# FFN2 and FFN3 as seven half-block products a unit, with weight sums on GpSimd

## What is computed

```python
# FFN2: D_FF = 2816 (22 tiles of 128)
x = _residual(x, _swiglu(_modnorm(x, g[4], m[6], m[7]), ffn2_w1, ffn2_w3, ffn2_w2), g[5], m[8], 0.5)
def _swiglu(h, w1, w3, w2):
    return (jax.nn.silu(h @ w1) * (h @ w3)) @ w2
...
# FFN3: D_FF_2 = 4096 (32 tiles)
u = rmsnorm(x, norm_mlp_g) @ w_up
x = x + jnp.square(jax.nn.relu(u)) @ w_down
```

## Time and profile before

| | |
|---|---|
| runs | 3321.23, 3317.41, 3318.78 us (median 3318.78) |
| span of the profiled execution | 3320.6 us |
| PE busy | 3122.6 us, 94%, 9082 matmuls |
| PE weight load busy | 1592.1 us, 48% |
| DVE, ACT, POOL busy | 766.2, 433.0, 56.2 us |
| PE L281 `normed` x ring | 4208 matmuls, 1648.2 us |
| PE L281 `big` x ring | 2368 matmuls, 950.3 us |
| HBM | 68 GB/s over the span |

### The profile page before, as it was taken

One profiled execution on the slowest core, in us unless ns is written; L12 is line 12 of the kernel. 1 busy time (PEld: TensorE's weight loads), 2 busy tenths in 40 slices (PEclk: granted clock), 3 DMA queues, 4 the chain that ended last, 5 costly groups with the idle time before them and its releaser, 6 DMA issues.

```text
span 3320.6 us, 22877 instructions
## 1 busy us (share of the span) xinstructions
PE 3122.6 (94%) x9082; PEld 1592.1 (48%) x9082; DVE 766.2 (23%) x1393; ACT 433.0 (13%) x908; POOL 56.2 (2%) x98
## 2 busy tenths in 40 slices
PE   3999999997999999998999998997889999999998
PEld 1555555553557366443444443753434444444443
DVE  6222225004016443002000004108540001110012
ACT  2000000002014243002000001004330001000001
POOL 0000000000002000000000000000000000000000
PEclk8999999998999999998999999998899999999999
DMA  5222223111110100221221121110012121222211
GB/s 244 89 102 103 103 95 144 44 60 38 51 39 1 39 10 29 76 83 51 76 76 72 64 80 63 64 65 13 26 45 76 76 76 64 76 76 76 75 45 57
DMA packets 38460, 227.69 MB, mean 69 GB/s; under 512 B 4208, under 2 KB 4464, under 8 KB 20848
## 3 DMA queue, kind: packets, MB, share of 16 engines
q1 hardware_dynamic: 28736, 181.17, 14.7%
q0 software_dynamic: 8928, 39.85, 3.2%
q10 hardware_dynamic: 720, 5.61, 0.4%
HBM read 224.51 MB, written 2.10 MB: 68 GB/s over the span
## 4 chain that ended last, share of the span: by engine, by line
PE 90%; DVE 6%; ACT 1%; DMA 1%; issue 1%; ACTq 0%; DVEq 0%
PE banks L281 80%; PE banks L386 1%; PE banks L541 1%; PE banks L461 1%; PE banks L534 1%; DMA consts_sb<-consts 1%; PE banks L333 1%; PE banks L290 1%; PE banks L679 1%; DVE rstd L1065 1%; DVE scratch_b L1082 1%; PE banks L451 1%; DVE p_embed L1115 1%; DVE stat L1370 0%; DVE residual L1088 0%
## 5 line engine op out<-in xcount | busy, mean ns | idle before, releaser
L281 PE MATMUL banks<-normed,weight_ring 128*128 128x512 f32 (+3 forms) x4208 | 1648.2, 553 | 53.4 <-ACT normed L769 34.0
L281 PEld LDWEIGHTS banks<-normed,weight_ring 128*128 128x128 f32 (+2 forms) x4208 | 802.4, 191 | 887.9 <-issue 841.0
L281 PE MATMUL banks<-big,weight_ring 128*128 128x512 f32 (+3 forms) x2368 | 950.3, 559 | 11.7 <-DVE big L1168 5.6
L281 PEld LDWEIGHTS banks<-big,weight_ring 128*128 128x128 f32 (+2 forms) x2368 | 444.5, 188 | 506.7 <-issue 480.5
L1115 DVE CUSTOM_DVE_ANT_0 p_embed<-big,rpb_rows 128x1024 f32<-128x1024 f32 x116 | 141.9, 1223 | 22.9 <-DMA big<-w_ada 15.5
L290 PE MATMUL banks<-scratch_a,consts_sb 128*128 128x512 f32 (+1 forms) x124 | 60.1, 621 | 65.5 <-ACT scratch_a L753 64.6
L782 ACT ACTIVATE scratch_b<-banks 128x512 f32<-128x512 f32 x44 | 26.3, 597 | 712.9 <-PE banks L281 712.9
L1075 DVE RECIPROCAL rstd<-rstd 128x512 f32<-128x512 f32 (+1 forms) x3 | 11.7, 3886 | 422.4 <-ACT rstd L757 422.4
L1165 DVE TENSOR_TENSOR scratch_a<-scratch_a,banks 128x512 f32<-128x512 f32 x16 | 11.0, 687 | 356.9 <-ACT scratch_a L815 356.9
L1143 DVE TENSOR_TENSOR big<-scratch_b,banks 128x512 f32 x22 | 15.1, 688 | 314.7 <-ACT scratch_b L782 314.7
L1148 DVE TENSOR_TENSOR big<-scratch_b,banks 128x512 f32 x22 | 15.1, 687 | 288.0 <-ACT scratch_b L782 288.0
(11 more groups left out here) (203 smaller groups left out, 1554.2 us busy)
## 6 DMA issues: line engine op xcount, KB each, us to landing
weight_ring<-weights SPq DMA_DIRECT2D x128, 1024.0 KB, 4.8
weight_ring<-weights SPq DMA_DIRECT2D x32, 704.0 KB, 3.9
big<-w_ada POOLq DMA_DIRECT2D x42, 512.0 KB, 3.9
weight_ring<-weights SPq DMA_DIRECT2D x16, 768.0 KB, 4.1
big<-w_ada POOLq DMA_DIRECT2D x4, 2048.0 KB, 25.1
rpb_rows<-w_ada POOLq DMA_DIRECT2D x14, 512.0 KB, 4.4
weight_ring<-weights SPq DMA_DIRECT2D x8, 640.0 KB, 3.9
residual<-xT ACTq DMA_DIRECT2D x2, 1536.0 KB, 19.7
```

The source lines that it names most:

```text
L281: ins = nc.tensor.matmul(o, w, r, start=start, stop=stop)
```

## The change

Each pair of output tiles of FFN2's and FFN3's products is made by Strassen's scheme in Winograd's form. The weights of a unit are four blocks (two output tiles by two halves of the inner channels, `kp` = 4 tiles each, or 3 in the last four units of FFN2's down product), the rows four blocks (two halves of the channels by two halves of 256 tokens). Seven products of `kp` matmuls of 256 columns stand where eight stood. There are 66 such units: 22 + 12 in FFN2 and 16 + 16 in FFN3.

- GpSimd makes the four sums of weight blocks of each unit (`weight_sums`, 128 x 512 elements each) into two sets of buffers.
- DVE makes the four sums of row blocks once for eight row tiles (`row_sums`, 4 x 256 elements a partition each), nine times in all.
- PE (`fast`) accumulates the seven products in three half banks a unit, with two sets in turn. ACT copies the first product (`fast_snap`), DVE adds the copy to what the second and the fourth left, and PE's products 4, 6 and 7 wait for these adds.
- The inner channels are cut into phases of eight hidden tiles (six at FFN2's end): up for a phase, then down for it, the partial results summed in SBUF (`Y1`, `Y2`, or straight into `X`).
- The last down units' results are squared in pairs of tiles, and PE sums them by four matmuls.
- SP's list (`STREAM`) gives the units in the new order, and a down unit gathers its blocks from two or four of the stored ones; the stored weights are the same.

```diff
+            def fast(v, rows, t, rows_sem=None, rows_at=0, t_at=None):
+
+                n, kp = unit_of(v)
+                za, zb, zc = zones(v)
+                a = [slot(n, i * kp * P, kp * P) for i in range(4)]
+                w = [SUMS[v % 2][:, i * kp * P:(i + 1) * kp * P] for i in range(4)]
+
+                def product(z, stationary, moving, opens):
+                    for p in range(kp):
+                        last = nc.tensor.matmul(z, stationary[:, p * P:(p + 1) * P], moving[:, p, :],
+                                                start=opens and p == 0, stop=p == kp - 1, skip_group_check=True)
+                    return last.then_inc(prod, 1)
+
+                def raw(j, l):
+                    return rows[:, j * kp:(j + 1) * kp, l * HALF:(l + 1) * HALF]
+
+                def total(i):
+                    return t[:, i, 0:kp * HALF].rearrange("p (k t) -> p k t", k=kp)
+
+                begin(n)
+                if v >= 2:
+                    pe.wait_ge(c11, copied_upto(v - 2))
+                    pe.wait_ge(took, 5 * (v - 1))
+                for p in range(kp):
+                    if rows_sem is not None:
+                        pe.wait_ge(rows_sem, rows_at + p)
+                    last = mm(za, a[0][:, p * P:(p + 1) * P], raw(0, 0)[:, p, :], p == 0, p == kp - 1, p == 0)
+                last.then_inc(prod, 1)
+                pe.wait_ge(sums, v + 1)
+                if t_at is not None:
+                    pe.wait_ge(hts, t_at + 2)
+                product(zb, w[1], total(1), True)
+                product(zc, w[0], total(0), True)
+                if t_at is not None:
+                    pe.wait_ge(hts, t_at + 3)
+                pe.wait_ge(took, 5 * v + 1)
+                product(zb, w[2], total(2), False)
+                pe.wait_ge(snap, v + 1)
+                product(za, a[1], raw(1, 0), False)
+                if t_at is not None:
+                    pe.wait_ge(hts, t_at + 4)
+                pe.wait_ge(took, 5 * v + 2)
+                product(zb, a[3], total(3), False)
+                pe.wait_ge(took, 5 * v + 3)
+                product(zc, w[3], raw(1, 1), False)
...
-            up_rounds(up2, "up2", LAT, nb["ready"])
-            out_projection(down2, down2["free"], "down2", FF, HID, LAT, 11, (down2, (4, 5)))
+            fast_up(range(0, 8), nb, 0)
+            fast_up(range(8, 16))
+            fast_down(16, 0, HT, 8, 4)
+            fast_up(range(20, 26))
+            fast_down(26, 1, HT, 16, 8)
+            fast_down(30, 2, TH, 22, 12)
+            squares_total(sq2)
...
+            def squares_total(g):
+
+                pe.wait_ge(g["added"], 2 * g["turn"] + 2)
+                nc.tensor.matmul(bank[:, 6, :], ones, SQA[:, 0:S], start=True, stop=False)
+                nc.tensor.matmul(bank[:, 6, :], ones, SQA[:, S:2 * S], start=False, stop=False)
+                pe.wait_ge(g["done"], 4 * g["turn"] + 4)
+                nc.tensor.matmul(bank[:, 6, :], ones, SQB[:, 0:S], start=False, stop=False)
+                nc.tensor.matmul(bank[:, 6, :], ones, SQB[:, S:2 * S], start=False, stop=True).then_inc(g["used"], 1)
...
+            def fast_snap(v):
+
+                s1 = tmps(v % 2)[0]
+                act.wait_ge(prod, 7 * v + 1)
+                if v >= 2:
+                    act.wait_ge(took, 5 * (v - 1))
+                A(s1, zones(v)[0], ACT.Copy).then_inc(snap, 1)
+
+            def up2_units(vs):
+                for v in vs:
+                    u2, g1 = tmps(v % 2)[1], tmps(v % 2)[4]
+                    fast_snap(v)
+                    act.wait_ge(prod, 7 * v + 5)
+                    A(g1, zones(v)[0], ACT.Silu).then_inc(c11, 1)
+                    act.wait_ge(took, 5 * (v + 1))
+                    A(u2, u2, ACT.Silu).then_inc(silued, 1)
+
+            def up3_units(v0, i):
+                if i >= 2:
+                    act.wait_ge(prod, 7 * (V_DOWN3[i - 2] + 4))
+                for j in range(4):
+                    fast_snap(v0 + j)
+                    act.wait_ge(prod, 7 * (v0 + j) + 5)
+                    A(HR[i % 2][:, 2 * j, 0:HALF], zones(v0 + j)[0], ACT.Copy).then_inc(c11, 1)
+
+            def last_down(v0, rows, g):
+                for m in range(4):
+                    fast_snap(v0 + m)
+                    if m >= 1:
+                        squares(v0, m - 1, rows, g)
+                squares(v0, 3, rows, g)
+
+            def squares(v0, m, rows, g):
+                act.wait_ge(took, 5 * (v0 + m + 1))
+                if m >= 2:
+                    act.wait_ge(g["added"], 2 * g["turn"] + m - 1)
+                A((SQA if m == 0 else SQB).rearrange("p (k t) -> p k t", k=2), rows[:, 2 * m:2 * m + 2, 0:S],
...
+            def row_sums(dst, rows, kp):
+
+                def raw(j, l):
+                    return rows[:, j * kp:(j + 1) * kp, l * HALF:(l + 1) * HALF]
+
+                def total(i):
+                    return dst[:, i, 0:kp * HALF].rearrange("p (k t) -> p k t", k=kp)
+
+                at = row_sums_done[0]
+                V.tensor_tensor(total(0), raw(0, 1), raw(0, 0), ALU.subtract).then_inc(hts, 1)
+                dve.wait_ge(hts, at + 1)
+                V.tensor_tensor(total(1), raw(1, 1), total(0), ALU.subtract).then_inc(hts, 1)
+                V.tensor_tensor(total(2), raw(1, 1), raw(0, 1), ALU.subtract).then_inc(hts, 1)
+                dve.wait_ge(hts, at + 2)
+                V.tensor_tensor(total(3), raw(1, 0), total(1), ALU.subtract).then_inc(hts, 1)
+                row_sums_done[0] += 4
+
+            row_sums_done = [0]
+
+            def fast_heads(v, last22):
+
+                s1, u2, u3, _, _ = tmps(v % 2)
+                _, zb, zc = zones(v)
+                dve.wait_ge(dve_c, chain[0])
+                dve.wait_ge(prod, 7 * v + 2)
+                dve.wait_ge(snap, v + 1)
+                V.tensor_tensor(u2, zb, s1, ALU.add).then_inc(took, 1)
+                dve.wait_ge(prod, 7 * v + 4)
+                V.tensor_tensor(u3, zb, s1, ALU.add).then_inc(took, 1)
+                dve.wait_ge(took, 5 * v + 2)
+                V.tensor_tensor(last22, zc, u3, ALU.add).then_inc(took, 1)
+                dve.wait_ge(took, 5 * v + 3)
+
+            def fast_c21(v, dst):
+                dve.wait_ge(prod, 7 * v + 6)
+                V.tensor_tensor(dst, zones(v)[1], tmps(v % 2)[0], ALU.add).then_inc(took, 1)
+
+            def fast_c12(v, dst):
+                dve.wait_ge(prod, 7 * v + 7)
+                return V.tensor_tensor(dst, zones(v)[2], tmps(v % 2)[1], ALU.add).then_inc(took, 1)
+
+            def up2_unit(v, f):
+                _, u2, u3, x22, g1 = tmps(v % 2)
+                dst = HR[f // PHASE % 2][:, f % PHASE, :]
+                if f >= 2:
+                    dve.wait_ge(hid, f - 1)
+                fast_heads(v, x22)
+                fast_c21(v, u3)
+                dve.wait_ge(took, 5 * v + 4)
+                dve.wait_ge(c11, copied_upto(v))
+                mark(V.tensor_tensor(dst[:, 0:HALF], u3, g1, ALU.mult))
+                fast_c12(v, u2)
+                dve.wait_ge(silued, f + 1)
+                V.tensor_tensor(dst[:, HALF:S], x22, u2, ALU.mult).then_inc(hid, 1)
+
+            def up3_unit(v, hr, t):
+                fast_heads(v, hr[:, t + 1, HALF:S])
+                fast_c21(v, hr[:, t + 1, 0:HALF])
+                fast_c12(v, hr[:, t, HALF:S])
+                dve.wait_ge(took, 5 * v + 5)
+                dve.wait_ge(c11, copied_upto(v))
+                rows = hr[:, t:t + 2, :]
+                V.scalar_tensor_tensor(rows, rows, 0.0, rows, ALU.max, ALU.mult).then_inc(hid, 1)
+
+            def down2_first(v, o):
+                fast_heads(v, Y2[:, o + 1, :])
+                fast_c21(v, Y1[:, o + 1, :])
+                fast_c12(v, Y2[:, o, :])
+
+            def down_add(v, o, old1, old2, new1, new2):
+
+                _, u2, u3, x22, _ = tmps(v % 2)
+                fast_heads(v, x22)
+                link(V.tensor_tensor(u2, u2, old2[:, o, :], ALU.add))
+                mark(V.tensor_tensor(new2[:, o + 1, :], x22, old2[:, o + 1, :], ALU.add))
+                dve.wait_ge(prod, 7 * v + 5)
+                mark(V.tensor_tensor(new1[:, o, :], zones(v)[0], old1[:, o, :], ALU.add))
+                fast_c21(v, u3)
+                dve.wait_ge(took, 5 * v + 4)
+                mark(V.tensor_tensor(new1[:, o + 1, :], u3, old1[:, o + 1, :], ALU.add))
+                fast_c12(v, new2[:, o, :])
+
+            def add_squares(g, m):
+                dve.wait_ge(g["done"], 4 * g["turn"] + m + 1)
+                V.tensor_tensor(SQA, SQA, SQB, ALU.add).then_inc(g["added"], 1)
...
+            dve.wait_ge(nb["ready"], KC)
+            row_sums(TH, H, 4)
+            for f in range(8):
+                up2_unit(f, f)
+            dve.wait_ge(hid, 8)
+            row_sums(HT, HR[0], 4)
+            for f in range(8, 16):
+                up2_unit(f, f)
+            for m in range(4):
+                down2_first(16 + m, 2 * m)
+            dve.wait_ge(prod, 7 * 20)
```

(146 more changed lines are left out.)

142 lines of the change are left out of this document (94 added, 48 removed).

## The result

| | before | after |
|---|---|---|
| median of the runs | 3320.0 us | 3263.0 us |
| ratio | | 0.982, interval 0.9806 to 0.9834 |
| span of the profiled execution | 3320.6 us | 3261.0 us |
| PE busy | 3122.6 us | 3027.8 us |
| DVE, ACT, POOL busy | 766, 433, 56 us | 1029, 446, 416 us |

The change makes the kernel 57 us faster, where 52 us slower was forecast, and the time lies outside the range. The row sums, the norms, the slow clock and the ends of the down products cost time, as named; the wait inside a unit and the turns outside the row sums cost PE nothing. The gain is twice what the prediction counted.

The account below looks back on a forecast made before the run. PE was taken as the bound; -60.1 + 5.3 + 29.5 + 13 + 16 + 1 gave +4.7 us (3323 us), and 49 for turns gave +53.7, forecast 3372 us; range 3306 to 3410 us.

Parts of the forecast that it names:

- The row sums: Seven DVE calls between units in FFN2 and FFN3 stall PE for 29.5 us, before any waiting for GpSimd.
- the norms: Behind two norms, product 2 needs all rows and two sums of them: 6.4 us each, 13 us.
- the slow clock: After each of seven PE stalls the clock restarts at half speed: 7 x 2.3 = 16 us, bounds 0 and 21.
- the ends of the down products: Both down products end about 0.5 us later each, by an ACT square over 1024 elements: 1 us.
- the wait inside a unit: PE waits 0.04 us twice in each of 66 units for DVE to read banks: 5.3 us, bounds 0 and 13.
- the turns outside the row sums: DVE and GpSimd alternate at up3 multiplies (8.5 us), down units (7) and up2 (2); 49 us with row sums.
- The gain: Fewer matmul columns in FFN2 and FFN3, shorter sums of squares and removed idle pieces: -60.1 us together.
- the cost of a matmul: In FFN2 and FFN3, 0.4292 us for 512 columns and 0.2158 for 256, so the units save 53.6 us.
- the sums of squares: After each down product, 4 matmuls of 512 columns instead of 8: 3.4 us less in all.
- the idle pieces: Two PE waits of 1.5 us, where a down product waits for the last hidden block, go: 3.1 us.
- GpSimd: Four weight sums a unit at 1.3 us each take 5.4 us with waits, needed 6.7 us later: no hold-up by itself.
- rival 3: GpSimd becomes the bound, PE waiting 0.4 us a unit ahead of product 2: 26 us more, 3398 us; chance 0.10.

Follow-up runs that it names:

- the spread one: Changed kernel with the seven row-sum calls between units cut into four 256-element subtractions, behind the third add of each of the next four units: 3213.3 us, ratio 0.9673.
- the last but one kernel: The kernel with row-sum calls cut into small subtractions, these moved from behind each unit's third add to ahead of its first: 3282.5 us, ratio 0.9883.

## Why the prediction was wrong

- **What was wrong: the cost of a matmul.** The step read the spacing of the rows (0.4292 us for 512 columns, 0.2158 for 256) as the time of a `matmul` in the code, and multiplied by counts from the code (16 and 28 a unit). The rows come in pairs: 704 rows for 352 matmuls stood in the very window that the prediction quoted, and the loop over eight tiles and two weights shows as 32 rows a unit. The same window contradicts the prediction's 6.87 us a unit: 22 of them are 151 us, and the window lasts 306.8. With the pair, the matmuls save 107.2 us instead of 53.6, the sums of squares 6.9 instead of 3.4, and with the idle pieces 117 instead of 60. The run with two matmuls less a unit shows the cost by itself. The two kernels without the seven stalls agree: the spread one is 110.8 us below before, 6 short of 117, and it still has the two norms' gaps. The Trainium skill ("FP8 and Floating Point Precision", TensorE Precision Notes) states that true fp32 takes four passes through the array. If a pass takes one cycle a column, an estimate from this is 4 x 512 columns at 2.4 GHz, 0.853 us; 0.858 us is measured for 512 columns, so this case agrees.
- **The wait inside a unit** was put at 5.3 us and costs nothing. With products of 1.73 us PE loads for product 4 at 3 x 1.727 - 0.216 = 4.96 us after the unit's start, which is 1575.54 in the unit shown, and the first add ends at 1574.71, 0.8 us earlier; the unit is 56 x 0.2158 us exactly. The same slip put DVE's latest free moment at 1.93 us. By the same working it is 4.96 - 0.05 - 0.43, some 4.5 us. (The expectation of the last but one kernel took 3.6, the moment at which product 2's result is out.)
- **Row sums.** 61 us of stalls were forecast (29.5 and 31.5 for the turns), 32.3 came. The place and the number, seven, were right. The call behind f=7 takes 7.7 us under turns, where 4.85 + 4.5 was said, and the slack is some 2.5 us longer (4.5 against 1.93). Turns are most of the cost: with GpSimd's sums cut, 7.0 of the 32.3 us are left.
- **The clock**: 16 us forecast, some 12 to 13 measured.
- **The norms**: 13 us forecast; two gaps of 3.4 us are seen, and making the sums by pairs gives back 5 by the medians, which the intervals do not settle. The spread kernel lacks 6 us of the 117 by the medians and 8 by the spans, for norms and ends together, where 14 were forecast.
- **The ends**: 1 us forecast. Before its four matmuls over the squares PE waits 1.65 us at the end of each down product, for DVE's sum of squares (L1428); in the kernel before it waited not at all and 0.71 us there, so the ends cost 2.6 us more. How the 6 to 8 us split between norms, clock and ends wasn't tried.

```profile
1978.44 1.12 PE L482 MATMUL banks<-scratch_a,consts_sb 128*128 128x512 f32 x2 [1.65 <-DVE scratch_a L1428]
```

- **GpSimd**: a sum takes 1.27 us alone; the groups' means hold the waiting of L1826 to L1828:

```profile
L1826 POOL TENSOR_TENSOR big<-weight_ring 128x512 f32<-128x512 f32 x62 | 101.3, 1634 | 0.0
L1825 POOL TENSOR_TENSOR big<-weight_ring 128x512 f32<-128x512 f32 x62 | 78.7, 1270 | 1190.8 <-PE banks L430 517.1 <-DMA weight_ring<-weights 430.7 <-issue 243.0
```

  The 5.4 us a unit have 12 us to lie in. It is no bound, and rival 3 was far off.
- **Turns**: taken, rightly, but at the row sums alone they cost time; the other 17.5 us of the 49 (in-place multiplies and adds) came to nothing, since no other wait for DVE stands inside the products. A DVE instruction with two SBUF inputs and a GpSimd one that reads SBUF exclude each other for the whole instruction, as the Trainium skill has it ("SBUF — State Buffer", SBUF: two separate sides), and the pairs of ends above agree. The same small subtractions cost nothing within the measurement behind the third add, and 69 us ahead of the first, the slow clock that follows included.

With the right cost of a matmul and the measured length of a call the sum of the prediction would have been -117 + 32 + 16 + 13 + 1, about -55 us (32 for the stalls: 61, less 7 x 2.5 of slack and 7 x 1.65 of the shorter call), against -57 measured. That it comes so near is in part luck: the clock and the norms are put too high in it and the ends too low.

## What to carry to other kernels

Before a spacing of rows is multiplied by a count from the code, divide the rows of one stretch by the instructions that the code issues there; here that one division changes the sign of the forecast. Then hold the length of a stage that comes out against the one in the trace. A product that is handed from PE to DVE and back wants DVE's other work behind the handover, not ahead of it, in small pieces, and where GpSimd isn't reading. And a stall of 4 to 5 us costs about 2 us more here in the slow clock behind it, so that filling it with idle matmuls paid even with nothing else changed.
